# Splitting the weight chunks of both attention stages with casting and adding transfers

## What is computed

```
# first block, dilated_layer: 24 query heads in 3 groups, and a gate z
qz = h @ w_in                                   # 1024 -> 4096: 32 tiles of 128 outputs
q = rms_norm(q, q_norm_g) * (HEAD_DIM ** -0.5)
o, lse = dilated_group_attn(q[:, :, hs], kb, vb, slopes[hs], window, d)   # per group
y = o * jax.nn.silu(z)
return x + gate * (y @ w_out)                   # "bo": 1024 -> 1024, 8 tiles

# second block, hybrid_mixer: 8 heads of 64, a convolution of width 31, and gates
y_a = chunked_attention(q, k, v, rel_table) @ w_attn_out
y_b = conv_module(c_in, ...)
gates = jax.nn.sigmoid(g + gate_bias)           # g: 1024 -> 2048, 16 tiles of 128 outputs
merged = gates[..., :D_MODEL] * y_a + gates[..., D_MODEL:] * y_b
return merged @ w_out
```

## Time and profile before

| | |
|---|---|
| three executions | 1919.17, 1919.83, 1920.21 us |
| profiled execution, its own time | 1920.68 us |
| profiled execution, span of the trace | 1919.0 us |
| mean granted clock of TensorE, as a share of full speed | 0.989 |
| TensorE, VectorE, ScalarE, GpSimd busy | 95%, 55%, 38%, 3% |
| first attention ("qz") | 509 to 772 us |
| "bo" | 772 to about 830 us |
| second attention ("gates") | 1316 to 1452 us |

### The profile page before, as it was taken

How to read it: one execution, slowest core, us unless ns; L and a number is a source line. 1 busy time by engine, 2 the same in 40 slices (tenths; PEclk the granted TensorE clock), 3 DMA queues, 4 the chain that set the end, 5 groups by cost and what they waited for, 6 DMA issues and landing times.

```text
span 1919.0 us, 22232 instructions
## 1 busy us (share of the span) xinstructions
PE 1829.7 (95%) x8618; PEld 1493.1 (78%) x8618; DVE 1047.5 (55%) x1498; ACT 736.6 (38%) x1008; POOL 52.7 (3%) x103
## 2 busy tenths in 40 slices
PE   4999999989999999999999999999999999999998
PEld 3788888856877777778888887987667888888887
DVE  6336666458566667654444314699876453333223
ACT  4445554224355555432322214323453342223212
POOL 1000001000000000100000000000000000000000
PEclk8999999989999999999999999999999999999999
DMA  8346565521322212233333232232223323342321
GB/s 331 134 131 190 175 176 173 152 77 66 88 66 66 66 50 62 66 94 104 88 111 97 101 108 88 78 120 66 66 66 105 93 76 100 88 120 77 121 88 66
DMA packets 246679, 201.10 MB, mean 105 GB/s; under 512 B 6386, under 2 KB 225860, under 8 KB 245572
## 3 DMA queue, kind: packets, MB, share of 16 engines
q1 hardware_dynamic: 238048, 166.25, 29.3%
q0 software_dynamic: 8064, 33.56, 5.0%
q10 hardware_dynamic: 484, 0.16, 0.0%
HBM read 197.83 MB, written 2.11 MB: 104 GB/s over the span
## 4 chain that ended last, share of the span: by engine, by line
PE 77%; DVE 13%; ACT 5%; issue 3%; DMA 1%; DVEq 0%; SPq 0%; POOL 0%; ACTq 0%; POOLq 0%
PE acc L700 13%; PE acc L701 13%; PE acc L702 13%; PE sc L1066 6%; DVE s_s_row L2166 4%; PE acc L1066 3%; DVE s_w_low L1830 2%; PE tr L1066 2%; ACT s_w_high L1326 2%; PE ob L1066 2%; PE misc L1066 2%; PE sc L701 1%; PE sc L702 1%; DMA s_ada_w<-in_a_ada_w 1%; PE sc L700 1%
## 5 line engine op out<-in xcount | busy, mean ns | idle before, releaser
L1830 DVE TENSOR_TENSOR s_w_low<-s_raw,s_w_high 128x2048 fp32r<-128x2048 f32 (+1 forms) x149 | 337.1, 2263 | 356.2 <-ACT s_w_high L1326 356.1
L1326 ACT ACTIVATE s_w_high<-s_raw 128x2048 fp32r<-128x2048 f32 x151 | 284.6, 1885 | 205.0 <-PE acc L1066 167.7
L700 PE MATMUL acc<-s_h_high,s_w_high 128*128 128x512 f32 x880 | 345.1, 392 | 1.6 <-DVE s_sg L2402 1.6
L701 PE MATMUL acc<-s_h_low,s_w_high 128*128 128x512 f32 x880 | 342.5, 389 | 0.0
L702 PE MATMUL acc<-s_h_high,s_w_low 128*128 128x512 f32 x880 | 342.5, 389 | 0.0
L700 PEld LDWEIGHTS acc<-s_h_high,s_w_high 128*128 128x128 f32 x880 | 165.3, 188 | 37.6 <-issue 4.0
L702 PEld LDWEIGHTS acc<-s_h_high,s_w_low 128*128 128x128 f32 x880 | 165.2, 188 | 34.2
L701 PEld LDWEIGHTS acc<-s_h_low,s_w_high 128*128 128x128 f32 x880 | 165.3, 188 | 33.7 <-issue 0.2
L1702 ACT ACTIVATE s_hid_high<-s_hd 128x512 fp32r<-128x512 f32 x44 | 27.8, 632 | 219.3 <-DVE s_hd L2411 119.0
L891 PE MATMUL acc<-s_h_high,s_w_high 128*128 128x512 f32 x256 | 107.6, 420 | 2.2 <-DVE s_w_low L1830 1.4
L700 PE MATMUL acc<-s_b_high,s_w_high 128*128 128x512 f32 x224 | 91.5, 409 | 11.7 <-DVE s_b_low L1879 7.7
(11 more groups left out here) (460 smaller groups left out, 3354.4 us busy)
## 6 DMA issues: line engine op xcount, KB each, us to landing
s_raw<-in_a_w_in SPq DMA_DIRECT2D x48, 512.0 KB, 5.0
s_raw<-in_ffn_w_gate SPq DMA_DIRECT2D x44, 512.0 KB, 4.0
s_raw<-in_ffn_w_up SPq DMA_DIRECT2D x44, 512.0 KB, 5.2
s_raw<-in_ffn_w_down SPq DMA_DIRECT2D x40, 512.0 KB, 4.1
s_raw<-in_w_in SPq DMA_DIRECT2D x36, 512.0 KB, 4.4
s_raw<-in_b_w_in SPq DMA_DIRECT2D x32, 512.0 KB, 4.8
s_ada_w<-in_b_ada_w POOLq DMA_DIRECT2D x24, 512.0 KB, 5.0
s_ada_w<-in_a_ada_w POOLq DMA_DIRECT2D x8, 1024.0 KB, 12.4
```

The lines of the kernel that those rows point to most:

```text
L700: pe.matmul(bank[b][:, :], w_high[:, o:o + P], hi, start=(k == 0), stop=False, skip_group_check=grouped)
L701: pe.matmul(bank[b][:, :], w_high[:, o:o + P], lo, start=False, stop=False, skip_group_check=grouped)
L1326: act.activation(w_high[:, part], raw[:, part], ACT.Copy).then_inc(w_high_ready, 1)
L1830: dve.tensor_tensor(w_low[:, w], raw[:, w], w_high[:, w].bitcast(F32), ALU.subtract).then_inc(w_ready, 1)
```

## The change

For 24 chunks (chunks 1 to 15 of "qz", 0 and 1 of "bo", 1 to 7 of "gates": `BY_QUEUE`) the split is made another way. GpSimd's queue issues a transfer that copies `raw` to `w_high` and casts it from float32 to fp32r on the way. ScalarE writes the negated chunk to `w_low` (rounded to fp32r, so it is -`w_high`) where it wrote `w_high` before. Then GpSimd's queue issues a second transfer, which adds `raw` onto `w_low`. TensorE, and SP for the next load, wait for both transfers in place of `w_ready`. VectorE's 22 subtractions in "qz" and "gates" and GpSimd's two in "bo" are gone. Three hardware loops that issue or wait for such chunks are written out, and counters of `w_ready` are shifted by the number of moved chunks. The diff, cut to its core:

```diff
+BY_QUEUE = [C0["qz"] + j for j in range(1, 16)] + [C0["bo"], C0["bo"] + 1] + [C0["gates"] + g for g in range(1, 8)]
...
             def wait_slot(q, s):
 
-                if not isinstance(q, int) or q > 0:
-
-                    sp.wait_ge(x_landed, 16 * TT)
-                    sp.wait_ge(w_ready, 2 * q + s - 1)
+                before = 2 * q + s - 2
+                if isinstance(q, int) and q == 0:
+                    return
+                sp.wait_ge(x_landed, 16 * TT)
+                if isinstance(q, int) and before in BY_QUEUE:
+                    sp.wait_ge(high_cast[s], 16 * slot_use(before))
+                    sp.wait_ge(low_added[s], 16 * slot_use(before))
+                elif isinstance(q, int):
+                    sp.wait_ge(w_ready, by_engines(before))
+                else:
+                    sp.wait_ge(w_ready, 2 * q + (s - 1 - moved))
...
+            def by_queue(c, tiles):
+
+                s = c % 2
+                w = slice(s * SLOT, (s + 1) * SLOT)
+                pool.wait_ge(w_landed[s], 32 * (c // 2) + 32)
+                pool.wait_ge(tile_ready, tiles)
+                pool.dma_start(w_high[:, w], raw[:, w]).then_inc(high_cast[s], 16)
+                pool.wait_ge(low_negated, BY_QUEUE.index(c) + 1)
+                pool.dma_start(w_low[:, w], raw[:, w], accum_op=ALU.add).then_inc(low_added[s], 16)
+
+            for j in range(1, 16):
+                by_queue(C0["qz"] + j, T0["qz"] + 2 * (j - 1))
             for s in range(2):
-                pool.wait_ge(w_high_ready, C0["bo"] + s + 1)
-                w = slice(s * SLOT, (s + 1) * SLOT)
-                pool.tensor_tensor(w_low[:, w], raw[:, w], w_high[:, w].bitcast(F32), ALU.subtract).then_inc(w_ready, 1)
+                by_queue(C0["bo"] + s, TILES_END["qz"] - 2 * (1 - s))
...
-            tile_sum()
+            for g in range(1, 8):
+                if g == 4:
+                    tile_sum()
+                by_queue(C0["gates"] + g, T0["gates"] + 2 * (g - 1))
...
             def chunk(c):
-                pe.wait_ge(w_ready, c + 1)
+                if isinstance(c, int) and c in BY_QUEUE:
+                    pe.wait_ge(high_cast[c % 2], 16 * slot_use(c))
+                    pe.wait_ge(low_added[c % 2], 16 * slot_use(c))
+                elif isinstance(c, int):
+                    pe.wait_ge(w_ready, by_engines(c))
+                else:
+                    pe.wait_ge(w_ready, c + (1 - moved))
...
+            def negated(c, tiles):
+
+                s = c % 2
+                w = slice(s * SLOT, (s + 1) * SLOT)
+                act.wait_ge(w_landed[s], 32 * (c // 2) + 32)
+                act.wait_ge(tile_ready, tiles)
+                act.activation(w_low[:, w], raw[:, w], ACT.Copy, scale=-1.0).then_inc(low_negated, 1)
...
+            negated(C0["qz"] + 1, t0)
             for s in range(NQ):
...
-                    if t is not None and t % 2 == 0 and t < 4 * NQ - 2:
-                        next_high(q0 + t // 4, t // 2 % 2, t0 + t)
+                    if n == 1:
+                        negated(C0["qz"] + t // 2 + 2, t0 + t + 1)
                 if s == 0:
                     act.wait_ge(dist_ready, GROUPS)
                 head_bias(s)
+                if s < NQ - 1:
+                    negated(C0["qz"] + 2 * s + 3, t0 + 4 * s + 4)
             a = NQ - 1
-            high_part(bo_q, 0, t0 + 4 * NQ - 2)
             stores(a - 1, 3)
             row_exp(a, 0)
             leave(4 * NQ - 1)
-            high_part(bo_q, 1, TILES_END["qz"])
+            negated(C0["bo"] + 1, TILES_END["qz"])
...
-                if n % 4 == 0:
+                if n == H2 * TT - 4:
                     next_high(q0 + n // 8, n // 4 % 2, t0 + n // 2)
+                elif n % 4 == 0:
+                    negated(C0["gates"] + n // 4 + 1, t0 + n // 2)
                 conv_norm(n - LN_AT)
...
-                    if low is not None:
-                        next_low(*low)
-                        low = None
...
-                if n % 4 == 1:
+                if n == H2 * TT - 3:
                     next_low(q0 + n // 8, n // 4 % 2)
```

More of the change, by code:

```diff
@@ L84, with by_engines, slot_use @@
 HALF_CHUNKS = {C0[name] + c for name in ("dn1", "dn2") for c in range(2)}
+BY_QUEUE = [C0["qz"] + j for j in range(1, 16)] + [C0["bo"], C0["bo"] + 1] + [C0["gates"] + g for g in range(1, 8)]
+def by_engines(c):
+    return c + 1 - sum(m <= c for m in BY_QUEUE)
+def slot_use(c):
+    return sum(m <= c and m % 2 == c % 2 for m in BY_QUEUE)
+MOVED_QZ, MOVED_GATES = 17, len(BY_QUEUE)
 def crossed(name, t):
@@ L330, in build @@
         w_high_ready, w_ready = sem("w_high_ready"), sem("w_ready")
+        high_cast = [sem("high_cast0"), sem("high_cast1")]
+        low_negated, low_added = sem("low_negated"), [sem("low_added0"), sem("low_added1")]
         tile_ready = sem("tile_ready")
@@ L449, in _ @@
         def _(sp):
+            moved = 0
             def wait_slot(q, s):
-                if not isinstance(q, int) or q > 0:
-                    sp.wait_ge(x_landed, 16 * TT)
-                    sp.wait_ge(w_ready, 2 * q + s - 1)
+                before = 2 * q + s - 2
[9 more added lines that the diff above has]
+                    sp.wait_ge(w_ready, 2 * q + (s - 1 - moved))
             def column(n0):
@@ L550, in _ @@
             q0 = C0["bo"] // 2
-            with sp.Fori(0, 2) as i:
+            for i in range(2):
                 for s in range(2):
                     chunk_wide(i + q0, s, W["b_out"], i * 512 + s * 2 * P)
+            moved = MOVED_QZ
             def ffn(l, post, pre=None):
@@ L583, in _ @@
             q0 = C0["gates"] // 2
-            with sp.Fori(0, 4) as i:
+            for i in range(4):
                 for s in range(2):
@@ L587, in _ @@
                     chunk_paired(i + q0, s, W["in2"], n0, W["in2"], n0 + D)
+            moved = MOVED_GATES
             q0 = C0["outs"] // 2
@@ L1824, in _ @@
             own = Chain(dve, dve_own)
+            moved = 0
             def low_part(q, s):
-                dve.wait_ge(w_high_ready, 2 * q + (s + 1))
+                if isinstance(q, int):
+                    dve.wait_ge(w_high_ready, by_engines(2 * q + s))
+                else:
+                    dve.wait_ge(w_high_ready, 2 * q + (s + 1 - moved))
                 w = slice(s * SLOT, s * SLOT + chunk_width(q, s))
@@ L2265, in _ @@
                         y_rest(s - 2)
-                    if t is not None and t % 2 == 0 and t < 4 * NQ - 2:
-                        low = q0 + t // 4, t // 2 % 2
             scale(a - 1, 3)
```

3 lines of the change are left out of this document (1 added, 2 removed).

## The result

| | before | after |
|---|---|---|
| median of four executions, each | 1919.62 us | 1890.66 us (1890.31 to 1893.48) |
| ratio, 95% interval | | 0.985 (0.984 to 0.986) |
| profiled execution, its own time | 1920.68 us | 1891.0 us |
| span of its trace | 1919.0 us | 1889.4 us |

The change gains 29 us.

What follows compares the result with a forecast made beforehand. TensorE, busy 95%, was taken as the bound, with about 28 us of its waits in question. Removal 17.2 + 7.2 = 24.4 us, less 3.6 us stall, 20.8 net: from 1920.7 to 1899.9, say 1900 us; range 1894 to 1936.

Steps and rivals of the forecast that it cites:

- Which waits go: First attention: TensorE's waits of 7.9, 4.6 and 1.4 us go, and two for scaled rows, 1.6 and 1.7: 17.2 us.
- "bo", 1.7 us: In "bo": TensorE's 1.72 us wait for VectorE's scaling, stretched beside GpSimd's subtraction, goes.
- The second attention, 7.2 us: Second attention: without the subtractions, 7.2 us of TensorE's 9.7 us of waits for scaled rows go; bounds 4.5 and 9.7.
- Three quarters: Second attention: the share of the 9.7 us of waits counted as removed, 7.2 us.
- The budget of 7.9 us: Chunks 4 to 14, even: the adding transfer has 7.9 us from the negation's end before TensorE wants the chunk.
- The stall of 3.6 us: First attention: TensorE waits 0.6 us for the adding transfer at each of six chunks, 3.6 us in all.
- Two passes: Adding transfer: source and target both read, 3.0 us each plus 2.5 us fixed, 8.5 us.
- The removal in "qz", 15.5 us: Stage "qz": removed waits of TensorE were to gain 15.5 us, before a stall of 3.6 us.
- Hidden entirely: Rival: the adding transfer takes at most 7.9 us, so the gain is 24.4 us, about 1896 us; chance 0.22.
- A: The adding transfer's time from negation to landing; likeliest 8.5 us, and 11.2 us would use up the whole gain.
- The queue rival: Rival: the cast ahead in GpSimd's queue delays the adding transfer to 14 us, 1947 us; chance above 11.6 us 0.25.
- Transfers held up by VectorE: Rival: each issue on GpSimd grows by some 0.5 us, stall 6.6 us, 1903 us; within a shared chance of 0.41.

Runs made afterwards that it cites:

- wait: Changed kernel plus an unused 1.9 us ScalarE copy where the cast stood, head slots 1 to 5, VectorE waiting for it without work: 1893.46 us.
- work: Changed kernel plus an unused 2.3 us maximum on VectorE at 13 places where the subtraction stood, without waiting for ScalarE: 1893.43 us.
- both: Changed kernel plus the unused ScalarE copy in head slots 1 to 5, VectorE waiting for it and then computing an unused maximum: 1905.44 us.
- the run with this part alone: Kernel before with only chunks 1 to 7 of "gates" split by the transfers, "qz" and "bo" as before: 1913.55 us.
- the halves: Changed kernel with each of the 48 transfers issued as two of 512 KB: 1892.98 us.
- the reversed order: Changed kernel with the adding transfer issued first on GpSimd's queue and the casting one behind it: 1915.55 us.
- the reordering: Kernel before, no transfers, with VectorE's subtraction at position n = 1 moved behind the score row: 1940.66 us.

## Why the forecast was right, and where it was wrong

**Which waits go: right for all but one.** The waits put down to ScalarE's squares and to the reciprocal were VectorE's subtraction at second hand. The runs with wait, work and both show this for the squares in five head slots, and for the reciprocal in part. The wait of 1.58 us for a scaled row in head slot 7 was forecast to go whole, and 0.75 us of it stayed.

**"bo", 1.7 us: right**, 1.9 us in the profile, 1.6 by the run that leaves the subtractions on GpSimd.

**The second attention, 7.2 us: right in size, in part by luck.** It is 7.2 us in the profile and 6.9 us by the run with this part alone. The waits of 1.57, 1.80 and 1.70 us have gone, the first one of 1.39 has stayed. But the listed waits fell by 6.3 us only, from 9.7 to 3.4, and not below the 3 us named as a sign. "Three quarters" took too much idle time, at too low a price for each microsecond of it.

**The budget of 7.9 us: right**, 7.85 in head slot 5.

**The stall of 3.6 us: wrong, and the first term that was mis-sized.** "Two passes" at 3.0 us each and 2.5 us fixed gave 8.5 us; the transfer took 7.35 with the wait for the negation, and there was no stall. The fixed part was nearly right (2.2, and 0.3 from the negation's end to the issue). The data took 4.8 us, not 6.0. That is 1.8 times the cast's 2.6 us (2.0 times by the landings of the halves), so "two passes" fits, though no run shows what the transfer reads and writes. But a pass within SBUF is the cast's 2.6 us, 403 GB/s, and not the 3.0 us (350 GB/s) that I took from loads out of HBM. The Trainium skill (DMA: Bandwidth & Descriptors, "Where 436 GB/s comes from") has these two limits apart, 358 GB/s for HBM and 435 within SBUF, and the trace agrees with the second. The estimate of 4.2 us from the Trainium skill (Collectives: The Full Stack, "The bandwidth ceiling: the fold count and why AG ≠ RS ≠ AR") was nearer to the measured 4.8 us, 0.6 below, than the two passes at HBM's rate, 1.2 above.

**The removal in "qz", 15.5 us: wrong, and the second.** It was 19.8 us. I had added up the idle times that the list of waits shows, and counted each at its own length. Of the 15.5 us, 14.7 went. Five head slots gave 2.53 us each for 2.04 listed (+2.5 us together), head slot 1 gave 3.4 for 2.9, and head slot 7 gave 3.5 for 1.6; head slot 0 was 0.2 shorter with no wait listed. In head slot 7, before, TensorE waited 1.58 and 1.08 us, and was then granted 0.50 to 0.78 of its clock for 4 us; after, it stayed at 1.00, which is 1.7 of the 3.5 us. The windows of the kernel before, behind those waits:

```profile
762.91:763.91 1.00, 1.00 (x4) 0.87 (x5) 0.40 (x2) 1.00 (x1) 0.00 (x0) 0.52 0.00 0
763.91:764.91 1.00, 1.00 (x4) 0.81 (x3) 0.49 (x3) 0.97 (x4) 0.00 (x0) 0.50 0.00 0
764.91:765.91 1.00, 1.00 (x4) 0.71 (x4) 0.87 (x4) 1.00 (x1) 0.00 (x0) 0.50 0.00 0
765.91:766.91 1.00, 1.00 (x5) 0.80 (x4) 0.35 (x3) 0.78 (x5) 0.00 (x0) 0.78 0.00 0
```

**The sum.** Forecast 24.4 - 3.6 = 20.8 us. Measured on the traces: 19.8 + 1.9 + 7.2 = 28.9, and 0.7 elsewhere, of 29.6 us. The lower end of the range, "all waits gone", took listed idle time for the most that could be won, and so was no bound. Even all of the 28 us "in question" were no bound: 29 were won with 1.7 + 3.4 us of such waits still there. Two slips don't touch the forecast: by its own formula "no change" begins at A = 10.8 us and not 10.6, and the 0.02 for "no effect" was counted as slower.

**The rivals.** "Hidden entirely" is what happened to the transfer, at a larger removal than it assumed. The queue rival has its mechanism confirmed by the reversed order. In the kernel's own order its sign, a cast that lands later than the negation, did appear in half of the pairs, and cost nothing there. Transfers held up by VectorE: the casts' issue took 545 ns in the median, as short as the shortest, with VectorE at work beside; the adding ones took 876 (870 to 905). But what stood beside them was mostly score rows and maxima. A scaling met an issue only three times, for 0.13 us at most, and a copy of VectorE lay over one cast's issue, which took 551 ns. So the rule of the Trainium skill (SBUF — State Buffer, "Who interferes with whom"), by which descriptors written by GpSimd suffer beside VectorE in its two-port modes, was hardly put to the test here. On GpSimd's arithmetic the trace agrees with it: VectorE's scaling took 2.16 us beside the subtraction and 0.45 us without it.

**Open.** Why TensorE's busy time is 0.49 us longer in a head slot with two short waits at full clock was measured, and taken apart only at the two waits. Of the clock in head slot 7 it is shown that it falls in some kernels and not in others after the same two waits, and not what decides it.

## What to carry to other kernels

An engine's wait can be charged to the wrong work. When an idle time ends with a late producer, go back on that producer's queue to the last instruction that itself waited, and ask what stood between. Here 2.3 us of subtraction cost time because they began when the data for the critical row arrived, and cost nothing when they began 2 us sooner. Before counting on a move, look at which tile needs the moved result: it was the next one, and the reordering lost 20 us.

Idle time listed at a wait was a lower bound of its price here. Short waits gave back 1.05 to 1.35 times it, waits of 3.4 to 4.5 us about 1.4 to 1.5 times where the granted clock was halved behind them, and 1.1 times in the one head slot where it was not. A transfer's time is fixed part plus data: take the rate from a transfer between the same memories.

## What the runs showed of the hardware

- A casting transfer of 1 MB within SBUF took 4.2 us at the shortest, by its half 1.6 us fixed and 2.6 us of data; an adding one took 7.0 us, 2.2 fixed and 4.8 of data. Issuing them took GpSimd 0.55 and 0.88 us, and 0.86 us for a cast right behind an adding one.
- Splitting them in halves gave no earlier end of the whole, and the first half 2.4 us sooner.
- After 3.3 to 3.4 us without a matmul TensorE ran 3.4 us at 1.2 GHz in six cases of seven (subtraction behind the row), after 2.0 us in two of four (reversed order), after 1.26 us in none. After 0.75 and 1.08 us with 0.44 us of work between, it did in seven profiles and did not in five.
- The profile put a wait for a transfer down to "issue" in one kernel and to the transfer in another.
